# A decoder step in fp32 on one core: the first eight pages, the key tables and two batches' recent keys of the sample stage are fetched during the prompt attention

## The reference, cut to what matters

```
def reference(...):
    ...
        xp, kvp, winp, hrp, hip = _layer_prompt(xp, lw, slopes)
        kv_past = cache_kv[l][page_table].reshape(n_seq, n_pages * page, 4, N_KV, HEAD_DIM)
        xs, kvs, wins, hrs, his = _layer_sample(xs, kv_past, state_win[l], ...)

def _layer_sample(x, kv_past, win_buf, h_re, h_im, lw, slopes):
    q, kv, gates, u, mg = _in_proj(x, g_mix, w_in)
    kv4 = jnp.concatenate([kv_past, kv[:, :, :4]], axis=1)
    o_c, o_s = _cmp_sel_attend(q, pos, kv4, pe, pool, phi, slopes)   # pooled keys, and the 16 best blocks of 64 keys
    kvw = jnp.concatenate([win_buf, kv[:, :, 4:]], axis=1)
    o_w = _window_attend(q, pos, kvw[:, :, 0], kvw[:, :, 1], kpos, slopes)
    o = gates[0] * o_c + gates[1] * o_s + gates[2] * o_w
    ...
    y = _merge_ffn(x, o, y_ssm, mg, w_attn_out, w_glu, w_out, g_ffn, w_gate, w_up, w_down)
```

## Time and profile before

| what | value |
|---|---|
| time, median of 3 runs | 2252.19 us (2247.28 to 2254.45) |
| time of the profiled execution | 2258.55 us |
| its span, first to last instruction | 2256.7 us |
| mean granted TensorE clock | 0.965 |
| PE busy | 2116.3 us (94%) |
| DVE, ACT, POOL busy | 1085.4, 806.3, 112.8 us |
| prompt attention, by PE's first and last instruction | 558.7 to 725.3 us |
| sample stage, from the barrier to PE's first glu matmuls | 730.6 to about 991 us |

### The profile page before, as it was taken

The page is one execution under the profiler, slowest core; times in us unless marked ns, Lnnn a source line. Parts: engine busy times, 40 slices in busy tenths (PEclk is TensorE's granted clock), DMA queues, the critical chain, the costliest instruction groups (busy, mean ns, idle before and its releaser), DMA issues.

```text
span 2256.7 us, 38952 instructions
## 1 busy us (share of the span) xinstructions
PE 2116.3 (94%) x15836; PEld 1972.8 (87%) x15836; DVE 1085.4 (48%) x1740; ACT 806.3 (36%) x1164; POOL 112.8 (5%) x168
## 2 busy tenths in 40 slices
PE   8999798898997689989999999999999999999997
PEld 6999787777896355569999989999999999999997
DVE  4333477843464155545564444444444444444443
ACT  5223232242343255554434333322332333233343
POOL 1000011000000112210001100000000000000011
PEclk9999898999997799999999999999999999999998
DMA  7645643443342978846445545455545554555543
GB/s 175 196 130 149 152 118 96 112 110 109 107 148 85 409 272 328 335 156 229 143 152 146 152 127 149 136 152 163 149 140 142 166 149 140 146 164 149 147 125 115
DMA packets 553109, 364.88 MB, mean 162 GB/s; under 512 B 64753, under 2 KB 528194, under 8 KB 552162
## 3 DMA queue, kind: packets, MB, share of 16 engines
q1 hardware_dynamic: 471186, 314.13, 45.3%
q10 hardware_dynamic: 80096, 41.25, 6.8%
q0 software_dynamic: 1712, 7.97, 0.9%
HBM read 345.58 MB, written 23.63 MB: 164 GB/s over the span
## 4 chain that ended last, share of the span: by engine, by line
PE 55%; issue 6%; DMA 2%; SPq 2%; DVE 2%; ACT 1%; POOL 1%; POOLq 0%; DVEq 0%; ACTq 0%
PE bank L282 52%; SPq L1627 1%; DMA arena<-in_cache_kv_dram 1%; SPq L1637 1%; DMA w_raw<-in_w_glu_dram 1%; DVE w_lo L258 1%; DMA xT<-out_dram 0%; PE bank L1819 0%; POOL ysT L1695 0%; PE bank L1794 0%; ACT w_hi L253 0%; PE bank L1784 0%; PE bank L1774 0%; PE bank L2038 0%; DVE arena L2397 0%
## 5 line engine op out<-in xcount | busy, mean ns | idle before, releaser
L282 PE MATMUL bank<-hx,w_hi 128*128 128x320 f32 x3072 | 677.3, 309 | 5.6 <-DVE w_lo L258 5.6
L258 DVE TENSOR_TENSOR w_lo<-w_raw,w_hi 128x2048 fp32r<-128x2048 f32 (+2 forms) x222 | 463.9, 2090 | 351.4 <-ACT w_hi L253 351.3
L282 PE MATMUL bank<-act,w_hi 128*128 128x320 f32 x2432 | 539.9, 311 | 4.9 <-DVE w_lo L258 4.9
L282 PEld LDWEIGHTS bank<-hx,w_hi 128*128 128x128 f32 x3072 | 514.4, 188 | 6.1 <-DVE w_lo L258 6.1
L253 ACT CAST w_hi<-w_raw 128x2048 fp32r<-128x2048 f32 (+2 forms) x222 | 385.6, 1737 | 324.8 <-PE bank L282 317.5
L282 PE MATMUL bank<-hx,w_lo 128*128 128x320 f32 x1536 | 475.2, 309 | 0.0
L282 PEld LDWEIGHTS bank<-act,w_hi 128*128 128x128 f32 x2432 | 408.2, 189 | 6.4 <-DVE w_lo L258 5.9
L282 PE MATMUL bank<-act,w_lo 128*128 128x320 f32 x1216 | 377.2, 310 | 0.0
L282 PEld LDWEIGHTS bank<-hx,w_lo 128*128 128x128 f32 x1536 | 288.9, 188 | 0.0
L663 PE MATMUL bank<-actr,half_hi 128*128 128x320 f32 x1024 | 242.5, 326 | 20.3 <-DVE half_lo L634 20.2
L282 PEld LDWEIGHTS bank<-act,w_lo 128*128 128x128 f32 x1216 | 229.6, 189 | 0.0
(11 more groups left out here) (384 smaller groups left out, 1896.9 us busy)
## 6 DMA issues: line engine op xcount, KB each, us to landing
arena<-in_cache_kv_dram SPq DMA_DIRECT2D x128, 512.0 KB, 7.0
w_raw<-in_w_gate_dram SPq DMA_DIRECT2D x44, 1024.0 KB, 5.2
w_raw<-in_w_up_dram SPq DMA_DIRECT2D x44, 1024.0 KB, 5.2
w_raw<-in_w_down_dram SPq DMA_DIRECT2D x64, 704.0 KB, 4.5
half_raw<-in_w_in_dram ACTq DMA_DIRECT2D x64, 512.0 KB, 4.2
w_raw<-in_w_in_dram SPq DMA_DIRECT2D x20, 1024.0 KB, 5.1
w_raw<-in_w_glu_dram SPq DMA_DIRECT2D x32, 512.0 KB, 5.1
w_raw<-in_w_out_dram SPq DMA_DIRECT2D x16, 1024.0 KB, 5.7
```

The lines of the kernel that those rows point to most:

```text
L258: nc.vector.tensor_tensor(w_lo[s][:, 0:job.kt * job.width], raw[s][:, 0:job.kt * job.width], w_hi[s][:, 0:job.kt * job.width].bitcast(F32) ...
L282: mm = pe.matmul(bank[:, 0:NT], w[s][:, at:at + P], x[:, kk, :], start=first and k == 0 and m == 0, stop=final and k == job.kt - 1 and m == 2)
```

## The change

It issues some of the sample stage's loads in the block before. In the prompt attention's SP program `ptab` is loaded first. After the window copy of batch 4 SP waits until the gate columns have used the split x, and then issues the first eight pages, `poolsel`, `kbs` and, for batches 0 and 1, recent keys, recent values and new rows. The pages and `kbs` go into `early`, which has the address of `actr`; the memory of the last block is laid out anew so that quads 1 and 0 and `kbs` stand at that same place. The recent keys go into `xT`, as before. The block's end waits for all 16 of these DMAs. In the last block SP begins with quad 2 of batch 0, `kbw` comes after quad 3, and the waits for what is already there are dropped. The weight buffers `w2` stand behind `act2` instead of before it, and the gate load of `gb[2]` waits for `y_split`.

```diff
+        ptab = sb("ptab", [P, NB * NPG], I32)
...
+        with ExitStack() as alias:
+            early = alias.enter_context(nc.sbuf_tensor("early", [P, 2 * KT * NT], F32))
         actr = kept.enter_context(nc.sbuf_tensor("actr", [P, 2, KT, NT], F32R))
...
+        EARLY_AT = 4
+        QP, RQ = 4, 4
+        NQUAD = NPG // QP
+        EARLY = 2 * QP
...
+        def load_page(sp, dst, n, landed):
+            at = sp.value_load(ptab[0:1, n:n + 1], min_val=0, max_val=n_pool - 1)
+            sp.dma_start(dst, page_rows[bass.ds(at, 1), :, :].rearrange("o t n -> (o t) n")).then_inc(S(landed), 16)
+
+        def load_recent_keys(sp, m, landed):
+            sp.dma_start(wns[m % 2], state_win[0, m].rearrange("(t p) a g d -> p t (a g d)", p=P)).then_inc(S(landed), 16)
+
+        def load_new(sp, m, landed):
+            sp.dma_start(vnews[m % 2][0:NQ, 0, :], kvr_sample[0, m, :, 3].rearrange("t g d -> t (g d)")).then_inc(S(landed), 16)
+            sp.dma_start(vnews[m % 2][0:NQ, 1, :], win_sample[0, m, WIN - NQ:WIN, 1].rearrange("t g d -> t (g d)")).then_inc(S(landed), 16)
...
             def _(sp):
+                sp.dma_start(ptab[0:1, :], page_table.rearrange("b g -> (b g)").rearrange("(o n) -> o n", o=1)).then_inc(S("ptab_landed"), 16)
...
                     sp.dma_start(win_sample[0, b, 0:WIN - NQ].rearrange("t a g d -> t (a g d)"),
                                  state_win[0, b, NQ:WIN].rearrange("t a g d -> t (a g d)")).then_inc(S("stored"), 16)
+                    if b == EARLY_AT:
+
+                        sp.wait_ge(S("ptab_landed"), 16)
+                        sp.wait_ge(S("w_used"), gates.n)
+                        for n in range(EARLY):
+                            q, j = n // QP, n % QP
+                            load_page(sp, early[:, ((1 - q) * QP + j) * 1024:((1 - q) * QP + j + 1) * 1024], n, "early_landed")
+                        sp.dma_start(poolsel, kbias[:, PAST + WIN + 2 * NQ:].rearrange("p (v c) -> p v c", v=2)).then_inc(S("early_landed"), 16)
+                        sp.dma_start(early[:, 8192:10240], kbias[:, 0:PAST]).then_inc(S("early_landed"), 16)
+                        sp.wait_ge(S("kv_stored"), 13 * 16)
+                        for m in range(2):
+                            load_recent_keys(sp, m, "early_landed")
+                            load_new(sp, m, "early_landed")
+                sp.wait_ge(S("early_landed"), (EARLY + 8) * 16)
...
+        def page_wait(eng, n):
+
+            loads = n // RP + (n % RP >= EARLY)
+            if loads:
+                eng.wait_ge(S(f"page_landed{n % RP}"), 16 * loads)
...
-                sp.dma_start(ptab[0:1, :], page_table.rearrange("b g -> (b g)").rearrange("(o n) -> o n", o=1)).then_inc(S("ptab_landed"), 16)
-                sp.dma_start(kbs, kbias[:, 0:PAST]).then_inc(S("kb_landed"), 16)
-                sp.dma_start(kbw, kbias[:, PAST:PAST + WIN + 2 * NQ]).then_inc(S("kb_landed"), 16)
-                sp.dma_start(poolsel, kbias[:, PAST + WIN + 2 * NQ:].rearrange("p (v c) -> p v c", v=2)).then_inc(S("kb_landed"), 16)
-                sp.wait_ge(S("ptab_landed"), 16)
...
-                for q in range(RQ):
+                for q in range(EARLY // QP, RQ):
                     load_quad(0, q)
+                sp.dma_start(kbw, kbias[:, PAST:PAST + WIN + 2 * NQ]).then_inc(S("kb_landed"), 16)
                 for t in range(NB - 1):
                     for q in range(NQUAD):
                         load_quad(t + 1, q)
-                    load_recent(t)
+                    if t >= 2:
+                        load_recent(t)
...
                 for c in range(3):
+                    if c == 2:
+                        pool.wait_ge(S("y_split"), 6)
                     gates(gb[c], KT + 4 * c, f"sgb_back{c}")
...
-                    pe.wait_ge(S(f"wn_landed{m % 2}"), 48 * (m // 2 + 1))
+                    if m >= 2:
+                        pe.wait_ge(S(f"wn_landed{m % 2}"), 48 * (m // 2))
...
-                pe.wait_ge(S("kb_landed"), 48)
                 pe.wait_ge(S("pw_ready"), 1)
...
+                    if m == 0:
+                        dve.wait_ge(S("kb_landed"), 16)
                     V.tensor_tensor(Sws[m % 2][:, 0:WIN], bank[:, :], kbw[:, NQ:NQ + WIN], ALU.add).then_inc(S("score_read"), 1)
...
-                dve.wait_ge(S("kb_landed"), 48)
```

More of the change, by code:

```diff
@@ L1262, in build @@
         gates = Gates(MG_S5, MG_ALL - MG_S5)
+        EARLY_AT = 4
+        QP, RQ = 4, 4
+        NQUAD = NPG // QP
+        EARLY = 2 * QP
+        x_flat, ys_flat = (buf[:, :, :].rearrange("p k n -> p (k n)") for buf in (xT, ysT))
+        wns = [x_flat[:, v * 2048:(v + 1) * 2048].rearrange("p (t n) -> p t n", t=4) for v in range(2)]
+        vnews = [x_flat[:, 4096 + v * 512:4096 + (v + 1) * 512].rearrange("p (a n) -> p a n", a=2) for v in range(2)]
+        poolsel = ys_flat[:, 0:2 * (P + 1)].rearrange("p (v c) -> p v c", v=2)
+        n_pool = cache_kv.shape[1]
+        page_rows = cache_kv[0].rearrange("n t a g d -> n t (a g d)")
+        def load_page(sp, dst, n, landed):
[6 more added lines that the diff above has]
+            sp.dma_start(vnews[m % 2][0:NQ, 1, :], win_sample[0, m, WIN - NQ:WIN, 1].rearrange("t g d -> t (g d)")).then_inc(S(landed), 16)
         with program() as block:
@@ L1528, in build, with held @@
         take = scratch()
-        take_x = scratch(xT[:, :, :].rearrange("p k n -> p (k n)"), KT * NT)
-        take_ys = scratch(ysT[:, :, :].rearrange("p k n -> p (k n)"), 8 * NT)
+        take_ys = scratch(ys_flat, 8 * NT)
         spare = (CAT["distp"][0], CAT["validcp"][1])
         take_c = scratch(cst[:, spare[0]:spare[1]], spare[1] - spare[0])
-        QP, RQ = 4, 4
         RP = RQ * QP
-        NQUAD = NPG // QP
         quad = [None] * RQ
+        for q in (1, 0):
+            quad[q] = take(QP * 1024).rearrange("p (j n) -> p j n", j=QP)
+        take(PAST)
+        kbs = early[:, 8192:10240]
+        first_quads = [early[:, (1 - q) * QP * 1024:(2 - q) * QP * 1024].rearrange("p (j n) -> p j n", j=QP) for q in range(2)]
         for q in (2, 3):
             quad[q] = take(QP * 1024).rearrange("p (j n) -> p j n", j=QP)
+        pageA = [quad[n // QP][:, n % QP, :] for n in range(RP)]
+        def held(at):
+            return first_quads[at] if at < EARLY // QP else quad[at % RQ]
         KTc = [take(2 * QP * P).rearrange("p (g k) -> p g k", g=2) for _ in range(2)]
[L1540 to L1545, removed]
         Ss2 = take(PAST + NQ)
@@ L1551, in build @@
         pq = [take(512) for _ in range(2)]
+        take_ys(2 * (P + 1))
         qst = [take_ys(2 * 64).rearrange("p (g r) -> p g r", g=2) for _ in range(2)]
         kbw = take(WIN + 2 * NQ)
-        poolsel = take_ys(2 * (P + 1)).rearrange("p (v c) -> p v c", v=2)
         pw = take(32).rearrange("p (v r) -> p v r", v=2)
@@ L1570, in build @@
         last.close()
+        with ExitStack() as alias:
+            aF = alias.enter_context(nc.sbuf_tensor("actF", [P, 2 * KT * NT], F32))
+        actr = phase.enter_context(nc.sbuf_tensor("act2", [P, 2, KT, NT], F32R))
         open_weights(phase, "w2")
         with ExitStack() as alias:
-            aF = alias.enter_context(nc.sbuf_tensor("actF", [P, 4 * KT * NT], F32))
-        actr = phase.enter_context(nc.sbuf_tensor("act2", [P, 2, KT, NT], F32R))
+            hF = alias.enter_context(nc.sbuf_tensor("hxF", [P, 2 * KT * NT], F32))
         hx = phase.enter_context(nc.sbuf_tensor("hx", [P, 2, KT, NT], F32R))
@@ L1636, in load_quad @@
                         n = at * QP + j
-                        sp.dma_start(pageA[n % RP], rows[bass.ds(page(b, q * QP + j), 1), :, :].rearrange("o t n -> (o t) n"))\
-                            .then_inc(S(f"page_landed{n % RP}"), 16)
+                        load_page(sp, pageA[n % RP], n, f"page_landed{n % RP}")
                 def load_recent(m):
[L1641 to L1650, removed]
-                for q in range(RQ):
+                    landed = f"wn_landed{m % 2}"
+                    sp.wait_ge(S("pv_used"), 6 * (m - 1) - 1)
+                    load_recent_keys(sp, m, landed)
+                    sp.wait_ge(S("pv_used"), 6 * (m - 1))
+                    load_new(sp, m, landed)
+                for q in range(EARLY // QP, RQ):
                     load_quad(0, q)
+                sp.dma_start(kbw, kbias[:, PAST:PAST + WIN + 2 * NQ]).then_inc(S("kb_landed"), 16)
                 for t in range(NB - 1):
@@ L1763, in turn_and_pool @@
                     for j in range(QP):
[L1764 removed]
+                        mm = pe.matmul(bank[32 * j:32 * (j + 1), :], pw.rearrange("p v r -> p (v r)"), held(b * NQUAD + q)[:, j, 0:512],
                                        start=True, stop=True)
```

16 lines of the change are left out of this document (5 added, 11 removed).

## The result

| | before | changed |
|---|---|---|
| median of 4 runs each | 2252.64 us (2247.28 to 2254.45) | 2225.69 us (2223.52 to 2229.83) |
| ratio | | 0.9884, 95% interval 0.9868 to 0.9901 |
| profiled execution, its span | 2258.55, 2256.7 us | 2226.62, 2224.8 us |
| mean granted clock | 0.965 | 0.975 |

The change takes off 27 us by the medians (26 by the ratio, with an interval of 22 to 30 us). The two spans differ by 31.9 us, more than the medians. Part of that lies ahead of the edits: POOL's first instruction of the last block, just behind the barrier, stands at 722.7 us instead of 730.6. The prompt attention already began 5.0 us sooner (553.71 and 558.68 us for POOL's first instruction), after an S5 scan whose code is the same. From 300 to 350 us the clock was 0.88 in the one execution and 0.97 in the other.

What follows compares the result with a forecast made beforehand. Transfers were taken to bound batches 0 and 1, PE the later ones. The profiled span of 2256.7 us less 26.5, plus fixed overhead, gave 2232.0; with the median 6.4 us lower, 2225.7 was predicted, range 2221 to 2238.

Steps and rivals of the forecast that it cites:

- The sum: Sample stage: PE's walk from the barrier has batch 2 begin at 773.4 instead of 799.88 us, 26.5 us sooner.
- The prompt attention costs nothing: Prompt attention: 18 us of new transfers fit and are through near 706 us, so this side costs 0.
- PE starts with the barrier: Sample stage: PE's first instruction needs only `pw_ready` and comes at 731.3 instead of 738.28 us.
- Batch 0, 19.6 us: Sample stage: four quads take 15.6 us, plus 4.0 us lost to 8 us at half speed; ends at 750.9 us.
- Batch 1, 22.5 us: Sample stage: parts of 7.9 us, 4.3 us and 10.7 us less about 0.4 of half clock; ends at 773.4 us.
- the forecast's own signs of being wrong: PE waits for batch 1's pages, the barrier moves, or the kernels' distance shrinks between batch 2 and the glu product.
- rival B: Sample stage: only the bytes are saved, or the clock stays down; gain 14 to 21 us, chance 0.13.
- Do the pages keep up: Sample stage: quads land every 5.0 to 5.1 us, 2 to 4 us ahead of need, so PE sets the pace.
- The fall of the clock behind batch 2's start: Half-clock piece after 799.9 us, 1.59 instead of 1.04 us per eight transposes; if it vanishes, the gain's upper end holds.
- What is won stays: After the early batches: later loads and dense layers hang on PE, so its gain before 800 us carries to the end.
- C: Batches 2 and 3: no spare DMA, recent keys late, gain taken back; less than 7 us or nothing remains, chance 0.04.
- D: Prompt attention: slow transfers, at 87 GB/s, hold up the barrier; 11 us slower, chance 0.03.

Runs made afterwards that it cites:

- e0_after: The changed kernel timed again, unaltered, against the kernel before: ratio 0.9895 (0.9873 to 0.9917).
- e5_late: The changed kernel with the early loads issued behind batch 7's window copy instead of batch 4's; ratio 0.9956 to the kernel before.
- e9_at6: The changed kernel with the early loads issued behind batch 6's window copy instead of batch 4's; ratio 0.9917 to the kernel before.
- e6_sixteen: The changed kernel with all 16 pages of batch 0 early instead of eight; ratio 0.9864 to the kernel before.
- e2_pages: The changed kernel with only pages and tables early, recent keys back in the last block; ratio 0.9951 to the kernel before.
- e3_keys: The changed kernel with only the recent keys early, pages and tables back in the last block; ratio 0.9935 to the kernel before.
- e10_both: Nothing early; recent keys of batches 0 and 1 both queued ahead of batch 1's quads; ratio 0.9969 to the kernel before.
- e4_order: Nothing early; only batch 0's recent keys queued ahead of batch 1's quads; ratio 0.9978 to the kernel before.
- e7_pages_order: Pages and tables early; recent keys in the last block, batch 0's ahead of batch 1's quads; ratio 0.9926 to the kernel before.
- e1_layout: The changed kernel's memory layout with no early loads, all back in the last block; ratio 0.9997 to the kernel before.

## Why the prediction was right, point by point

**The sum.** 26.5 us were forecast; 22 to 30 were measured, with marks of 24.3 and 25.4 us in two executions of the same kernel. That the predicted 2225.7 and the measured 2225.69 us agree so closely is luck: the marks stand 1 to 2 us below the forecast gain, single terms were off by up to 3 us, and the four runs of each kernel spread by 6 to 7 us. From the barrier to batch 2 the sum asked for 42.8 us (730.6 to 773.4) and 45.0 were measured (43.8 in e0_after).

- *The prompt attention costs nothing.* Right: the idle time around the barrier is 6.00 us in both executions of the change, and the block up to PE's last instruction took 163.6 and 161.1 us, where it took 166.6 before. e5_late and e9_at6 show the condition. The cover is the time between the last transfer and the end of the other engines; in these two the last DMA landed at 738.2 and 725.3 us and the barrier's mark came 2.5 and 2.8 us later, with losses of 14.0 and 1.5 us, so once it is gone each microsecond costs one. EARLY_AT = 4 left so much of it that its size was not tested: the DMA engines were idle again at 700 us, 17 us ahead of PE's last instruction. For e5_late I came to 10 us and it was 14; the copy that was still under way, which I had left out, is worth some 2.5 us of it (an estimate: 1 MB at 408 GB/s).
- *PE starts with the barrier.* Right: 0.6 us after the mark.
- *Batch 0, 19.6 us.* Measured 18.8 (723.34 to 742.18), though with 0.8 us of page waits. The half clock at the start lasted about 5 us instead of 8; the two partly cancel.
- *Batch 1, 22.5 us.* Measured 25.5 (742.18 to 767.71). This is the term that was too small, and all of it in its first part: up to the turning of the recent keys 10.8 us instead of 7.9, behind it 14.8 instead of 14.6. Two of its first pages were waited for, 1.2 us, and the clock fell again: eight pooling products took 1.94 us at 745.07 instead of 1.06. The forecast said that the clock would not fall again before 770 us and that batch 1's pages would be there 2 to 4 us ahead of PE; the margin was below zero. That PE waits for pages of batch 1 is one of the forecast's own signs of being wrong, and in small it came; it is rival B's mechanism, with 3 us instead of 9. In e0_after batch 1's pages were waited for too (1.2 us, 1.9 with the one page of batch 0) and the clock did not fall in it: its first compression took 0.71 us and not 1.17. It needed 24.0 us for the batch (741.81 to 765.77). e6_sixteen, where these pages were there, has 22.3 us (746.91 to 769.21), which is the forecast.
- *Do the pages keep up.* This step had the landings wrong. They were to come 7.9 us behind the barrier (quad 2) and 18.4 us (batch 1's first quad). By POOL's copies they came at 10.7 and 21.9 us, when PE had been ready for batch 1's since 19.5 (742.18), and in e0_after at 10.6 and 22.3:

```profile
733.38 1.04 POOL L1741 COPY arena<-arena 128x1024 f32<-128x1024 f32 x1 [8.16 <-DMA arena<-in_cache_kv_dram]
...
744.57 1.04 POOL L1741 COPY arena<-arena 128x1024 f32<-128x1024 f32 x1 [4.02 <-DMA arena<-in_cache_kv_dram]
```

The sum let the queue run at its full rate from the start. The trace has 260 GB/s from 724 to 732 us and 418 from 732 to 774. Quads 2 and 3 and batch 1's first then followed each other after 5.6 us, not 5.0.
- *The fall of the clock behind batch 2's start.* It came in the changed kernel (pooling 1.94 us at 768.93), as before, and in e0_after (transposes of 1.94 us at 765.77), and not in e6_sixteen.
- *What is won stays.* Right: the distance between the two kernels was 32.2 us at batch 2's start (799.88 and 767.71) and 31.9 us at the end. From the kernels of the table the gain at the mark and the gain by ratio agree.

**Rivals.** B's gain of 14 to 21 us lies below the measured interval, and that only the bytes count fell with e2_pages, e3_keys and e10_both; its waits for pages came, but small. C, that it is taken back later, does not happen here; but the mechanism is real where the keys of batch 1 aren't early (e4_order, e7_pages_order), and the change had avoided it by fetching two batches' keys. D, slow transfers in the prompt attention, fell: 347 GB/s from 679 to 703 us. The layout has no part in it (e1_layout).

Page and trace: the rate of 358 GB/s that the Trainium skill gives ("SBUF — State Buffer", the summary of rules for kernel authors) is below what these kernels moved, 413 and 420 GB/s in the changed kernel, and the measured rate decides.

**Where the gain comes from.** The two halves alone make 10.5 and 14.6 us, together 25.1, where both at once make 24.3 and 25.4: they add. Of the 14.6 us for the keys about half (7.5, e10_both) was a matter of the queue's order.

## What to carry to other kernels

Where one engine waits at the start of a transfer-bound stage, walk its work against the landings one by one; what a fetched byte is worth depends on which wait it stands in, and here 2.1 MB gave more than 5.4 MB. A small tensor behind a long row of big ones on the same queue is a wait of its own, and removing one such wait can uncover the next. An early fetch is free as long as everything in its queue, the copies ahead of it and behind it included, has landed before the other engines' end; from there each microsecond costs one. A walk against the landings has to allow for the start of the queue, here 260 GB/s in the first 8 us against 418 behind them.

## What the runs showed that I had not expected

- PE can be busy and have half clock for long. In the kernel before it was busy 15.3 of the 16 us from 700 to 716 us at clock 0.50. In the changed kernel at the end of the prompt attention (mostly products of 64 columns behind weight loads of 128):

```profile
703.00:717.00 14.00, 11.98 (x56) 11.77 (x56) 5.38 (x15) 1.56 (x4) 0.00 (x0) 0.50 0.22 74
```

- Issuing an 8 KB DMA held SP's queue for 3.46 us in the changed kernel and for 3.83 us in e5_late (both L1286, the second batch's rows), where the first batch's rows, three DMAs earlier, took 0.44 and 0.50. It came each time behind some dozen big transfers. No run here shows why.
- The same code ahead of the edits differed by 8 us between two executions (the barrier at 722.7 and 730.6 us), a third of the gain to be measured. A mark that starts at the stage's own barrier took most of that out.
